# The weights' ring of a two-block fp32 model kernel: four raw and six split slots, splits five ahead, and a reordered start and attention

## What is computed

```python
def first_block(x, ...):                 # DEPTH = 2 layers
    xn = rms_norm(x); h = xn @ w_in      # 7 projections: latent q/kv, differential q/k/v, grouped q/k/v
    # latent attention (6 heads), differential attention (4 heads, two maps each), grouped attention (6 heads)
    x = x + concat([o_a, o_b, o_c]) @ w_o
    gate, up = split(rms_norm(x) @ w_gate_up); x = x + (silu(gate) * up) @ w_down   # hidden 2816

def second_block(x, ...):                # 2 layers
    x = layer_norm(x)
    # neighbourhood attention and sliding-window attention, gated, each with its branch matrix, then w_out
    x = layer_norm(ALPHA * x + mixer(x))
    # layer 0: dense swiglu, hidden 2816; layer 1: 8 experts, hidden 3584, the best 2 of 8 for each token
    x = layer_norm(ALPHA * x + ffn_or_moe(x))
```

## Time and profile before

| | us |
|---|---|
| median of three runs | 2267.04 |
| the profiled execution | 2266.71 |
| its span, first to last instruction | 2264.9 |
| TensorE busy in the span | 2216.7 (98%) |
| VectorE busy | 1701.9 (75%) |
| ScalarE busy | 1486.2 (66%) |
| POOL busy | 217.4 (10%) |

### The profile page before, as it was taken

How to read it: one execution, slowest core, us unless ns; L and a number is a source line. 1 busy time by engine, 2 the same in 40 slices (tenths; PEclk the granted TensorE clock), 3 DMA queues, 4 the chain that set the end, 5 groups by cost and what they waited for, 6 DMA issues and landing times.

```text
span 2264.9 us, 31128 instructions
## 1 busy us (share of the span) xinstructions
PE 2216.7 (98%) x11616; PEld 1870.3 (83%) x11616; DVE 1701.9 (75%) x2435; ACT 1486.2 (66%) x2187; POOL 217.4 (10%) x136
## 2 busy tenths in 40 slices
PE   9899999899999999999999999999999999999998
PEld 8878888787888898888889888888888888888886
DVE  6866557876556547555647799999999999999998
ACT  6665446675444565444556687787878787888886
POOL 1430000340002330000160000000000000000000
PEclk9999999999999999999999999999999999999999
DMA  7426555425556545655644599999999999999996
GB/s 291 133 89 209 187 188 193 148 67 196 188 188 205 169 131 179 200 187 178 209 147 154 204 352 360 353 365 347 372 353 367 351 369 347 368 360 377 370 365 239
DMA packets 156845, 569.33 MB, mean 251 GB/s; under 512 B 18512, under 2 KB 18864, under 8 KB 156048
## 3 DMA queue, kind: packets, MB, share of 16 engines
q1 hardware_dynamic: 153600, 554.00, 69.2%
q0 software_dynamic: 3088, 13.27, 1.7%
HBM read 566.15 MB, written 1.05 MB: 250 GB/s over the span
## 4 chain that ended last, share of the span: by engine, by line
PE 75%; DVE 2%; ACT 1%; issue 0%; DVEq 0%; POOL 0%; ACTq 0%
PE bank L514 20%; PE bank L516 20%; PE bank L515 20%; PE bank L2280 3%; PE bank L2281 3%; PE bank L2282 3%; PE bank L1854 1%; PE bank L1075 1%; PE bank L2959 1%; PE bank L1090 1%; PE bank L1166 1%; PE bank L1017 1%; PE bank L2890 1%; DVE w_lo L451 0%; PE bank L2152 0%
## 5 line engine op out<-in xcount | busy, mean ns | idle before, releaser
L451 DVE TENSOR_TENSOR w_lo<-raw,w_hi 128x1024 fp32r<-128x1024 f32 x991 | 1194.7, 1224 | 276.2 <-ACT w_hi L445 243.9
L445 ACT CAST w_hi<-raw 128x1024 fp32r<-128x1024 f32 x1052 | 1098.8, 1052 | 313.6 <-PE bank L516 259.7
L514 PE MATMUL bank<-w_hi,x_hi 128*128 128x512 f32 (+2 forms) x2144 | 833.7, 389 | 6.3 <-DVE w_lo L451 5.0
L516 PE MATMUL bank<-w_hi,x_lo 128*128 128x512 f32 (+2 forms) x2144 | 822.9, 384 | 0.0
L515 PE MATMUL bank<-w_lo,x_hi 128*128 128x512 f32 (+2 forms) x2144 | 821.7, 383 | 0.0
L514 PEld LDWEIGHTS bank<-w_hi,x_hi 128*128 128x128 f32 x2144 | 403.1, 188 | 85.5 <-DVE w_lo L451 6.2
L516 PEld LDWEIGHTS bank<-w_hi,x_lo 128*128 128x128 f32 x2144 | 403.0, 188 | 78.6
L515 PEld LDWEIGHTS bank<-w_lo,x_hi 128*128 128x128 f32 x2144 | 403.5, 188 | 72.8
L451 POOL TENSOR_TENSOR w_lo<-raw,w_hi 128x1024 fp32r<-128x1024 f32 x61 | 146.8, 2410 | 571.3 <-ACT w_hi L445 546.9
L516 PE MATMUL bank<-w_hi,qk_l 128*128 128x512 f32 (+1 forms) x496 | 191.9, 387 | 0.0
L514 PE MATMUL bank<-w_hi,qk_l 128*128 128x512 f32 x448 | 178.5, 398 | 0.2 <-DVE w_lo L451 0.2
(11 more groups left out here) (284 smaller groups left out, 2037.8 us busy)
## 6 DMA issues: line engine op xcount, KB each, us to landing
raw<-in_stream SPq DMA_DIRECT2D x1052, 512.0 KB, 5.7
tab<-in_lngb POOLq DMA_DIRECT2D x5, 1024.0 KB, 5.0
arena<-in_rpb POOLq DMA_DIRECT2D x16, 256.0 KB, 6.6
tab<-in_rowv POOLq DMA_DIRECT2D x2, 640.0 KB, 10.3
X<-in_x SPq DMA_DIRECT2D x1, 1024.0 KB, 5.0
out_y<-X SPq DMA_DIRECT2D x4, 256.0 KB, 2.6
tab<-in_ropec POOLq DMA_DIRECT2D x2, 448.0 KB, 5.5
tab<-in_ropes POOLq DMA_DIRECT2D x2, 448.0 KB, 6.4
```

The lines of the kernel that those rows point to most:

```text
L445: nc.scalar.copy(w_hi[:, s % SPLIT, :], raw[:, slot, :]).then_inc(hi_done, 1)
L451: e.tensor_tensor(w_lo[:, s % SPLIT, :], raw[:, s % RAW, :], w_hi[:, s % SPLIT, :].bitcast(F32), ALU.subtract).then_inc(done, 1)
L514: pe.matmul(out, xh, wh, start=first, stop=False)
L516: return pe.matmul(out, xl, wh, start=False, stop=last)
```

## The change

Line numbers in the changed kernel are up to 13 higher. Its parts:
- `RAW` is 4 (was 8), `SPLIT` 6 (was 4), and so `AHEAD` 5 (was 3). The memory is the same: 16 slots of 4 KB a partition, since a split slot is two.
- X comes in two parts, left and right 512 columns, the left behind the unit matrix and the right behind the first half of weights. POOL waits for each and tells TensorE. The first split stands behind the first pair of blocks, the others follow as the code below shows.
- In the first block's attention, some of VectorE's and ScalarE's work stands elsewhere: a sum in `rotate`, `diff_blocks`, `latent_heads(0)`, and in `attention` the steps at which each engine runs `units` ahead or `aside` behind.
- In the second block POOL subtracts other halves, two or three later.

```diff
-RAW = 8
-SPLIT = 4
+RAW = 4
+SPLIT = 6
 AHEAD = SPLIT - 1
 PERIOD = RAW
...
-        own |= {mixer2_at(l), mixer2_at(l) + 1}
-    own.add(mixer2_at(0) + H_MIX2)
+        own |= {mixer2_at(l) + 3, mixer2_at(l) + 4}
+    own.add(mixer2_at(0) + H_MIX2 + 2)
...
-                if between is not None and b0:
-                    between(b0 // 2 - 1)
+                if between is not None and b0 != 2:
+                    between(max(b0 // 2 - 1, 0))
...
             if first:
+                for d in range(KD // 2 - 1, AHEAD):
+                    E.prologue(d)
                 keep_busy(E, 5, 7)
...
-                if E.kind == "act" and step in units_ahead:
+                if E.kind == "act" and step in act_ahead:
                     units(step)
...
-                ahead = step in units_ahead
-                if early and (E.kind == "pe" or ahead and E.kind == "dve" or not ahead and E.kind == "act"
-                              or E.kind == "pool"):
+                ahead = E.kind in ("pe", "pool") or E.kind == "act" and step not in act_ahead or (
+                    E.kind == "dve" and step in dve_ahead)
+                if early and ahead:
                     units(step)
-                aside(step)
+                if E.kind != "dve" or step not in aside_behind:
+                    if E.kind == "dve" and step - 1 in aside_behind:
+                        aside(step - 1)
+                    aside(step)
...
                 if part == 2 and c == C_DK and E.kind == "dve":
                     E.link(turned(E, x, 8, f, [(0, DQ)], heads_view(t1, 8, 64), z, 0))
-                    E.link(e.tensor_tensor(t1, t1, t2, ALU.add))
                 if part == 3 and c == C_DK:
                     if E.kind == "dve":
+                        E.link(e.tensor_tensor(t1, t1, t2, ALU.add))
...
             def beside_dv(hx):
-                if hx:
-                    diff_blocks(hx // 3 * 2, hx % 2)
+                if hx in (1, 2):
+                    diff_blocks(0, hx % 2)
...
             chunk(4, beside_dv, 0)
+            diff_blocks(2, 1)
             diff_blocks(2, 0)
-            latent_heads(0)
...
                 if step == 0:
+                    latent_heads(0)
                     latent_heads(1)
...
-            attention(E, maps, fill, act_copies=True, units=units, lag=2, units_ahead=(11,))
+            attention(E, maps, fill, act_copies=True, units=units, lag=2, act_ahead=(11, 13), dve_ahead=(10, 11),
+                      aside_behind=(11,))
...
             if E.kind == "pool":
+                for part in (x_left, x_right):
+                    e.wait_ge(part, 16)
+                    e.engine_nop().then_inc(tp_src, 1)
...
-            sp.dma_start(X[:, :, :], A["x"].rearrange("(t p) n -> p t n", p=P)).then_inc(x_in, 16)
-            sp.dma_start(ident[:, :], A["ident"]).then_inc(first_in, 16)
-            sp.dma_start(colg[:, :, :], A["colg"]).then_inc(first_in, 16)
+            left, right = slice(0, D // 2), slice(D // 2, D)
+            x = A["x"].rearrange("(t p) n -> p t n", p=P)
+            sp.dma_start(ident[:, :], A["ident"]).then_inc(ident_in, 16)
+            sp.dma_start(X[:, :, left], x[:, :, left]).then_inc(x_left, 16)
+            sp.dma_start(colg[:, :, :], A["colg"]).then_inc(colg_in, 16)
...
             for h in range(RAW):
                 load(h, h // 2, h % 2)
+                if h == 0:
+                    sp.dma_start(X[:, :, right], x[:, :, right]).then_inc(x_right, 16)
```

More of the change, by code:

```diff
@@ L114 @@
 TOTAL = MOE_AT + NE * H_EXP
-assert 2 * H_EXP % PERIOD == 0 and MOE_AT % 2 == 0 and TOTAL % 2 == 0
+assert 2 * H_EXP % PERIOD == 0 and 2 * H_EXP % SPLIT == 0 and MOE_AT % 2 == 0 and TOTAL % 2 == 0
 SOURCES = 2 + 4 * (2 * LAYERS - 1) + 4 * 2 * LAYERS + 4
@@ L357, in build @@
         c_in = sem("c_in")
-        x_in, first_in = sem("x_in"), sem("first_in")
+        x_left, x_right = sem("x_left"), sem("x_right")
+        ident_in, colg_in = sem("ident_in"), sem("colg_in")
         tab_in = sem("tab_in")
@@ L774, in unit, with attention @@
                 E.b2 = E.qk.at()
-        def attention(E, maps, aside, act_copies=False, units=None, lag=1, units_ahead=()):
+        def attention(E, maps, aside, act_copies=False, units=None, lag=1, act_ahead=(), dve_ahead=(), aside_behind=()):
             e = E.e
@@ L3068, in program @@
                 nc.scalar.activation(arena[:, WARM:WARM + 8], arena[:, 0:8], ACT.Square)
-                e.wait_ge(first_in, 32)
+                e.wait_ge(colg_in, 16)
             if E.kind == "dve":
@@ L3076, in program @@
                 E.link(e.memset(ms, 1.0))
-                e.wait_ge(first_in, 32)
-                e.wait_ge(x_in, 16)
-                e.engine_nop().then_inc(tp_src, 2)
+                e.wait_ge(colg_in, 16)
             if E.kind == "pe":
@@ L3083, in program @@
                     e.matmul(bank[7][:, 0:S], arena[:, 0:P], arena[:, P:P + S], start=True, stop=True)
-                e.wait_ge(first_in, 32)
+                e.wait_ge(ident_in, 16)
             if E.kind == "pool":
+                for part in (x_left, x_right):
+                    e.wait_ge(part, 16)
+                    e.engine_nop().then_inc(tp_src, 1)
                 e.wait_ge(half_set, 1)
```

## The result

The changed kernel takes 2603.8 us (median of three, 2601.92 to 2612.29) for 2267.04 before. The ratio is 1.150, with a 95% interval of 1.148 to 1.151. The profiled execution took 2603.8 us, its span is 2602.0.

The account below looks back on a forecast made before the run. TensorE was taken to bound the kernel, busy 2216.7 of 2264.9 us; in the experts the four-slot raw ring would become slower. 2266.7 + 289 - 5 - 0.5 = 2550 us, range 2430 to 2700.

Parts of the forecast that it names:

- the experts' term: Experts' stage: with four raw slots a half takes 1.91 us for 1.454, so 1266 us for 977, +289 us.
- The mechanism: Experts: a half takes (L + 2.48) / 4 us, L being issue to landing, if that is more than 1.454.
- The other dense stages: Feed-forward, output and first projection outside the experts: the ring's slower pace stays hidden, 0, at most +2 us.
- two more halves of cover can take them away: First 100 us: splits five ahead for three can remove TensorE's 2.6 us of waits for w_lo; at most -5 us.
- Splits ahead and order: Splits five ahead and the attention's reordering shorten TensorE's waits: -5 us together; the reordering's bounds were -12 and +5.
- The start: Kernel's start: X in two halves lets the first product begin near 10.8 us for 11.34, -0.5 us.
- POOL's new waits: Start: POOL's waits for X's two parts have only its tables behind them, which wait for the second cast anyway: 0.
- The ring keeps pace: Rival, experts: each load lands like a lone one, 3.5 us, TensorE stays the bound, 2261 us; chance 5%.
- It nearly keeps pace: Rival, experts: L = 3.7 to 4.4, 1.55 to 1.72 us a half, +50 to +165, about 2370 us; chance 8%.
- The queue stays slow: Rival, experts: L stays at 6.0 us, +429, 2690 us; chance 10%.
- The clock: Rival, experts: starved TensorE falls to 1.2 GHz for half the stage, 2.36 us a half, +609, 2870 us; chance 6%.
- the forecast's upper end: Experts: the forecast's case, L between 4.5 and 5.9 with 71% chance, was said to reach from 2441 to 2680 us.

Follow-up runs that it names:

- the kernel with half a subtraction: Against the changed kernel, VectorE subtracts only 512 of each half's 1024 columns in the experts: 2544.45 us, ratio 1.1239 to the kernel before.
- both rings back: Changed kernel with eight raw and four split slots, splits three ahead, its start and attention order kept: 2271.87 us, ratio 1.0032 to the kernel before.
- the ring alone: Kernel before with four raw and six split slots, POOL's halves moved and two splits added to the start; old start and order kept: 2611.56 us, ratio 1.1536.
- the loads of half the bytes: Against the changed kernel, each load in the experts brings only 64 of 128 partitions: 2318.74 us, ratio 1.0237 to the kernel before.

## Why the prediction was right, and where its sizes were off

The forecast was 2550 us, the kernel takes 54 more. 36 of these are the experts' term (325 us for 289), and 18 lie before the experts (12.3 us lost for 5.5 won).

**The mechanism was right, step by step.** Forecast were 471 casts in 900 us, there are 463; landings near 5.2, the median is 5.3; VectorE at 70%, it is 70.1; about 275 GB/s, it is 271; ScalarE's idle time ended by the load, 376 of 463 times; SyncE's waits stay. TensorE is busy for 83% and not 76: a matmul behind a gap or at the lower clock is counted longer, and 3,146 of them for 4,133 before are 76%, so the count and not the busy share was what the forecast spoke of.

**The experts' term was too small: 325 us against 289.** The first product of the stage and the last, before and after (start us, duration us):

```profile
1273.54 0.48 PE L514 MATMUL bank<-w_hi,x_hi 128*128 128x512 f32 x1
...
2251.19 0.39 PE L516 MATMUL bank<-w_hi,x_lo 128*128 128x512 f32 x1
```

```profile
1285.87 0.48 PE L515 MATMUL bank<-w_hi,x_hi 128*128 128x512 f32 x1
...
2588.46 0.39 PE L517 MATMUL bank<-w_hi,x_lo 128*128 128x512 f32 x1
```

977.7 us have become 1302.6. 663 halves at 1.94 in place of 1.91 are 20 us of the difference: L was 5.3 for 5.16, a tenth of a microsecond or so in each round, and every half pays a quarter of a round. The other 16 us the forecast had left out: it gave the stage nine ready halves but no way in and out. The tenth subtraction of the stage begins 9.7 us behind the first product, the 662 after it follow every 1.942 us, and the last product begins 7.4 us behind the last of them (8.7 behind the last cast, for 5.3 before).

**"The other dense stages: hidden, 0, at most +2" was wrong.** The stage begins 12.3 us later, where the forecast had it 5.5 earlier. Where a feed-forward of twelve matmuls runs, the step holds, and lined up not 0.1 us is lost between 200 and 350. There the rows answer:

```profile
L3181 SPq DMA_DIRECT2D raw<-in_stream x39: 327/328/328, 238.8 to 345.1; - x39
...
DMA to landing us min/median/max: 3.6/4.6/6.6
```

The loss lies in the first layer, between 20 and 60 us: 1.0 us behind at its first product, the changed kernel is 5.9 behind at 40 and 7.8 at 60. The other 4.5 us are what gains and losses of up to 3.4 us, in the attention above all, leave on balance. The forecast compared the mean pace of the halves with the ring's, and said that few short ones can't matter. But a ring of four with splits five ahead asks for a half while there is no slot for it. ScalarE and VectorE then stand at that split, with the evacuations that TensorE needs behind them in the same queues. ScalarE and VectorE there, and TensorE's waits up to 100 us, which answer to the earlier trace rows:

```profile
34.69 1.05 ACT L446 CAST w_hi<-raw 128x1024 fp32r<-128x1024 f32 x1 [2.27 <-DMA raw<-in_stream]
35.64 0.49 ACT L1310 ACTIVATE arena<-bank,small 128x288 f32<-128x288 f32 x1
```

```profile
35.77 1.23 DVE L452 TENSOR_TENSOR w_lo<-raw,w_hi 128x1024 fp32r<-128x1024 f32 x1 [2.09 <-ACT w_hi L446]
36.91 0.51 DVE L1315 TENSOR_SCALAR arena<-bank,small 128x288 f32<-128x288 f32 x1
```

```profile
PE bank L882 <- DVE small L896: 3.2, 2, 2.0
PE bank L1299 <- DVE x_lo L772: 2.9, 1, 2.9
PE bank L756 <- DVE arena L1315: 2.7, 1, 2.7
PE bank L536 <- POOLq L3094: 2.4, 1, 2.4
PE bank L515 <- DVE w_lo L452: 1.8, 1, 1.8
```

ScalarE stands 2.27 us at a cast with an evacuation behind it, VectorE 2.09 us at the subtraction of the same half, and TensorE waits 2.7 us for the evacuation behind that. Splits three ahead on the same ring of four lose 1 us until 60, for 6.8 (3.3 us behind at the first product, 4.3 at 60). A late first product might hide such a loss, but the kernel with half a subtraction, the changed kernel until the experts, is also 3.1 behind there, and loses 5.8 until 60 with its splits five ahead. So this is the price of five ahead: the step "two more halves of cover can take them away" had the sign wrong. It had asked what the cover hides, and not what stands in the queue behind a split that comes too early. At the experts' first product the kernel with splits three ahead has no lead left over the one with half a subtraction (10.1 us behind, and 10.3): it loses 7 us between 700 and 1200, where the change moves POOL's halves.

**Splits ahead and order, forecast at -5.** The order's part is real: 0.17%, 3.5 us by the runs and 3.0 by the traces, as the 2.4 and 1.7 us waits shrink or go. In both kernels 3 us are won between 60 and 80 and most of them given back until 100, by the waits that come in their place; the kernel with the order alone is 1.8 us ahead from 150 on and 3.0 at the experts. The changed kernel shows its gain only beside the ring alone, with 4.3 us at 150 and 0.9 at the experts' first product; that is the order's and the start's together. Its other half, the splits ahead, is the loss told above.

**The start, forecast at -0.5 with the first product near 10.8.** It begins at 12.31, for 11.34 before:

```profile
5.97 1.04 PE L536 MATMUL bank<-ident,X 128*128 128x128 f32 x8
...
9.41 1.09 PE L536 MATMUL bank<-ident,X 128*128 128x128 f32 x8 [2.40 <-POOLq L3094]
...
10.34 2.32 PE L1172 MATMUL bank<-X,ident 128*128 128x256 f32 x10
...
12.31 0.53 PE L515 MATMUL bank<-w_hi,x_hi 128*128 128x384 f32 x1
```

The left half's transposes start at 5.97, earlier than before. The forecast priced POOL's new waits at 0 because it asked only for what stands behind them on POOL; but TensorE waits for POOL's word, and the right half of X, now behind half a megabyte of weights, lands 2.4 us too late for it. The wait differs much from kernel to kernel with this start (2.4 us here, 4.4 with both rings back, its first product at 15.6), and the runs of the start alone show no loss. Its traced execution, the slowest of its eleven (2269.95), begins 0.8 us late and ends 3.2 late, so it does not show where the start is given back in the others, and no run was made for it.

**The rivals.** The ring keeps pace: no, it would need L = 3.5, which only the loads of half the bytes had. It nearly keeps pace, with L up to 4.4: no, L was 5.3. By the formula of the Trainium skill, "DMA: Bandwidth & Descriptors", section "Anatomy of one DMA — SWDGE (gpsimd) path", 512 KB would land after 3.2 us and 256 KB after 2.6, both estimates. Measured are 5.3 and 3.5 in this ring, so the traces agree with neither. The queue stays slow: no, L fell from 6.0 to 5.3 and with three slots to 4.7. The clock: in the experts it was granted at half for 109 us in 32 falls, mean 0.96. The chain in this stage has 1.0% of matmuls, so by it the falls cost next to nothing. The ring of four with splits three ahead points the same way: it had 34 us at half clock between 1300 and 2200, for 72 in the changed kernel, and was no faster. No run took the falls away. The price of this rival was also added up wrongly: by the forecast's own way of counting it is 663 x 2.36 - 977 = +588 and not +609, which changes nothing here. In the same way the forecast's upper end, L = 5.9, gives 2673 and not 2680.

## What to carry to other kernels

A ring of buffers has a round: issue to landing, then every reader of the slot in turn. Divide it by the slots and compare it with the pace of the engine that is the bound, and take the landing time at the load that the ring itself will make. Where the ring is the slower of the two, a slot's readers lie on the path though one was only 70% busy here, and TensorE's waits carry other names, those of the work queued behind the late split. And reaching further ahead in a queue that runs in order than the ring before it can deliver may cost instead of cover: it cost some 6 us in the first layer here, and saved some 14 in the experts.

## What the runs showed of the hardware

- The median landing time of a 512 KB load from SyncE's queue grows with the loads on the way: 3.7 us alone, 4.5 at 1.6, 4.7 at 2.0, 5.3 at 2.7, 5.5 at 2.8, 5.6 at 3.0, 6.0 at 4.1, when the stream moves 361 GB/s. A straight line from 4.5 to 6.0, as the prediction drew it, runs 0.1 to 0.3 us too low near three.
- Half the bytes on half the partitions: 3.5 us at 2.3 loads on the way.
- VectorE subtracts 512 columns in 0.693 us and 1,024 in 1.225 us.
